# Retention chunks rotated by GpSimd during attention instead of during the retention, with the rotated keys and the queries' high and low parts passed through device memory

## The chip, the core and the metric

One core of one Trainium2 chip runs one decoder layer. The metric is the device time of one execution in microseconds (us). The kernel before was timed in three runs.

## What is computed

```python
q, k = rotary(q), rotary(k) * (RET_QK ** -0.5)         # 4 heads of 256, 1024 tokens
for chunk in 8 chunks of 128 tokens, each head:
    inner = ((qc @ kc.T) * decay_in) @ vc
    cross = (qc @ R) * xi
    R = R * gamma_c + (kc * zeta).T @ vc
    out = inner + cross
y_ret = group_norm(out) * g_ret * silu(gate_ret)
y_mla = causal_attention(q_mla, k_mla, v_mla) * silu(gate_mla)   # 8 heads, 1024 tokens
merged = sigmoid(merge_mla) * (y_mla @ w_proj_mla) + sigmoid(merge_ret) * (y_ret @ w_proj_ret)
x = rmsnorm(x + gate * (merged @ w_out))
```

## The kernel before

Every product is made of three matmuls of float32r tiles: an operand is split into a high part (ScalarE copies it with rounding) and a low part (VectorE subtracts the high part from the whole), and the low-by-low product is left out. The program is written engine by engine, with semaphores set by hand, so the order of the instructions of an engine is the order of the Python loops. The stages that matter here are these.

**Attention** (`tensor_attention`), steps g = 0 to 63, one for each head and block of 128 queries. In a step TensorE does the scores, a piece of the *fill* (the projection of the retention's values, 32 units of 24 matmuls), the transposes of the step before's probabilities, and every second step the product with the values. `FILL_STEP` says how many fill matmuls stand in each step. When a fill unit is summed, ScalarE copies it with a factor to `v_stage` (`evict_fill`, L1587), VectorE makes its low part (L1998), and GpSimd stores both, 512 KB, to `v_ret` in device memory (`store_fill`, L1286). `v_slot` chooses the place in `v_stage`: units 1 and 31 have one of their own, the others take two places in turn. `evict_fill` waits until the last store from its place has landed (`v_stored`). Besides these stores GpSimd has no work until the last two steps.

**Retention** (`tensor_retention`), steps n = 0 to 31, one for each head and chunk. SyncE loads a chunk of q and k (`qk_raw`, L969) and of the cosine and sine tables (L971), `load_qk_chunk`, four steps ahead into three places. GpSimd rotates it in `rotate_chunk`: two products of 128x512 (L1277, L1279), then a difference and a sum of 128x256 (L1281, L1282). Chunks 0 and 1 are rotated before the last attention steps, the rest during the retention, and between them GpSimd forms `token_sums` of two finished chunks' outputs (L1231 to L1238), always one rotation or more behind. ScalarE then makes the high part of the rotated q and k (`high_qk`, L1594, 128x512) and VectorE the low part (`low_qk`, L1598, 128x512). TensorE transposes the keys (`turn_keys`, L2602), forms the scores (`inner_scores`, L2615 and L2616), the outputs (`outputs`), and the state (`state`); VectorE and ScalarE normalize the output (L2137 to L2148, L1620, L1630) and TensorE transposes it (`turn_outputs`, L2660). Between these TensorE has other matmuls to do: the last fill units, then the projection of `y_mla` (`fill_set`, L2504), whose operands `y_hi`/`y_lo` and weights VectorE and ScalarE split at the same time (L2183, L616).

Of the kernel before, what the change touches and what calls it, by code (L numbers as in the profile page):

```python
# [112 lines left out]
PAIR_CHUNKS = NT // 2  # L113
GROUPS_SPLIT = ((0, 1), (2,), (3,), ())
# [34 lines left out]
class Layer:  # L149
# [3 lines left out]
    def __init__(self, nc, sem, a, t, d, out, pools):  # L153
# [72 lines left out]
        self.qk_raw = [z("qk_raw_%d" % n, kb, [P, 6, P]) for n, kb in enumerate((56, 59, 4))]  # L226
        self.qk = z("qk_chunk", 62, [P, 2, 8, P], F32R)
        self.by_sine = [z("qk_by_sine_early", 98, [P, 4, P]), z("qk_by_sine", 0, [P, 4, P])]
# [84 lines left out]
    def semaphores(self, sem):  # L313
# [14 lines left out]
        self.x_late = sem("x_t_late_ready")  # L328
# [31 lines left out]
        self.roped = sem("k_pe_roped")  # L360
# [36 lines left out]
        self.gc_loaded = [sem("gate_chunk_loaded_%d" % n) for n in range(3)]  # L397
        self.qk_step = sem("qk_rotation_step")
# [19 lines left out]
        self.t_sums_done = sem("token_sums_done")  # L418
# [20 lines left out]
        self.out_hi_ready = sem("out_w_hi_ready")  # L439
# [255 lines left out]
    def v_slot(self, unit):  # L695

        return 2 if unit in (1, FILL_UNITS - 1) else unit % 2
# [225 lines left out]
    def sync_attention(self, sp):  # L923
        d = self.d
        parts = 0
        for g in range(STEPS + 4):
# [32 lines left out]
            if g == STEPS + 2:  # L959
                self.load_qk_chunk(sp, 2)  # L960
                self.load_qk_chunk(sp, 3)
# [44 lines left out]
    def sync_retention(self, sp):  # L1006
        d = self.d
        units = 0
        for n in range(CHUNK_STEPS):
# [14 lines left out]
            if n + 4 < CHUNK_STEPS:  # L1024
                self.load_qk_chunk(sp, n + 4)
# [24 lines left out]
    def store_sums(self, sp, k):  # L1050

        h, c = k // NT, k % NT // 2
        for done, tensor, which, slot in ((2, "sums_12", self.sums_12_stored, k % 4), (4, "sums_34", self.sums_34_stored, (k - 1) % 4)):
            sp.wait_ge(self.t_sums_done, 4 * (k // 2) + done)
# [121 lines left out]
    def gpsimd(self, pool):  # L1176
# [20 lines left out]
        for r in range(R_UP, R_V):  # L1197
            kind, i = SEQ[r]
            if kind == "b":
# [4 lines left out]
                nc.gpsimd.tensor_tensor(rot[:, 3, :], rot[:, 3, :], rot[:, 1, :], ALU.add).then_inc(self.rot_added, 1)  # L1204
        units = 0
        for g in range(STEPS + 4):
            while units < self.units_filled(g - 1):
                self.store_fill(pool, units)
                units += 1
            if g == STEPS - 2:  # L1210
                for n in range(2):
                    self.rotate_chunk(pool, n)
        for n in range(2, CHUNK_STEPS):
            if n == 9:
                for unit in range(units, FILL_UNITS):
                    self.store_fill(pool, unit)
            self.rotate_chunk(pool, n)
            if n >= 4 and n % 2 == 0:
                self.token_sums(pool, n - 3)
        for k in (CHUNK_STEPS - 3, CHUNK_STEPS - 1):  # L1220
            self.token_sums(pool, k)
        self.gpsimd_output(pool)

    def token_sums(self, pool, k):

        nc = self.nc
        before = 4 * (k // 2)
# [33 lines left out]

    def rotate_chunk(self, pool, n):

        raw, late = self.qk_raw[n % 3], int(n >= 12)
        by_sine = self.by_sine[late]
        cos, sin = (raw[:, c:c + 1, :].broadcast_to([P, 4, P]) for c in (4, 5))
        pool.wait_ge(self.chunk_loaded[n % 3], 32 * (n // 3 + 1))
        if n == 0:
            pool.wait_ge(self.v_stored[2], 16)
        elif n == 12:  # L1270
            for slot in range(3):
                pool.wait_ge(self.v_stored[slot], 16 * sum(self.v_slot(unit) == slot for unit in range(FILL_UNITS)))
        if n:
            pool.wait_ge(self.qk_step, 4 * n)
        if n >= 3:
            pool.wait_ge(self.out_done, n - 2)
# [1635 lines left out]
```

## Time and profile before

| | |
|---|---|
| runs | 1587.58, 1586.52, 1585.24 us; median 1586.52 |
| profiled execution | 1586.35 us, of which the span is 1584.5 us |
| TensorE matmul busy | 1540.6 us, 97% of the span |
| VectorE, ScalarE, GpSimd busy | 994.8, 667.4, 415.9 us |
| attention | about 753 to 1075 us of the span |
| retention | about 1075 to 1340 us of the span |

A busy time is the sum of an engine's instructions; time that the sequencer spends on semaphores is not in it. Times of places are microseconds from the start of the span. The rows of the trace stand in a section of their own below.

### The profile page before, as it was taken

The numbers are of one execution on the slowest core, as the hardware profiler recorded it, in microseconds if no ns is written. First come the engines' busy times: TensorE is split into PE (matmuls) and PEld (weight loads), VectorE is DVE, ScalarE is ACT, GpSimd is POOL, SyncE is SP. The second block draws the span as 40 slices with busy tenths as digits, with TensorE's granted clock in tenths as the row PEclk, the third lists the DMA queues.
The fourth block names the chain that finished last, engine by engine and source line by source line (L and its number), as shares of the span: only waits on it lengthen the run. The fifth ranks groups of instructions, "written<-read, shape, count | busy, mean of one in ns | idle before, by whom it ended". The sixth has DMA issues, their size and how long they took to land. (4 is left out here: it accounts for less than half of the span.)

```text
span 1584.5 us, 20414 instructions
## 1 busy us (share of the span) xinstructions
PE 1540.6 (97%) x7472; PEld 1287.2 (81%) x7472; DVE 994.8 (63%) x1629; ACT 667.4 (42%) x1144; POOL 415.9 (26%) x350
## 2 busy tenths in 40 slices
PE   5999999999999999999999999999899999999998
PEld 4788888888888888788888888887677888878886
DVE  6884444444444458752666665667988877799644
ACT  7553455543333353342343343434544444445311
POOL 0032233222322200200000000017778783522000
PEclk9999999999999999999999999999999999999999
DMA  9333232333323334699365554546988787889432
GB/s 381 104 136 113 107 113 107 114 108 118 120 106 107 94 108 156 260 413 339 134 207 176 173 200 172 186 140 229 307 268 265 255 271 240 297 286 309 156 107 80
DMA packets 154499, 299.55 MB, mean 189 GB/s; under 512 B 12048, under 2 KB 93072, under 8 KB 145696
## 3 DMA queue, kind: packets, MB, share of 16 engines
q1 hardware_dynamic: 137680, 265.80, 48.5%
q10 hardware_dynamic: 12080, 15.60, 2.9%
q0 software_dynamic: 4640, 16.84, 2.7%
q8 instruction: 60, 0.98, 0.3%
q14 instruction: 39, 0.32, 0.1%
HBM read 196.23 MB, written 100.93 MB: 188 GB/s over the span
## 5 line engine op out<-in xcount | busy, mean ns | idle before, releaser
L1894 DVE TENSOR_TENSOR w_form<-w_pair,w_form 128x512 fp32r<-128x512 f32 x150 | 116.3, 776 | 124.9 <-ACT w_form L1469 123.2
L1469 ACT ACTIVATE w_form<-w_pair 128x512 fp32r<-128x512 f32 x150 | 94.7, 632 | 216.8 <-PE p_banks L2433 211.7
L1551 ACT ACTIVATE prob<-p_banks,neg_max 128x128 f32<-128x128 f32 (+3 forms) x64 | 47.4, 741 | 183.1 <-DVE neg_max L2021 183.1
L1286 POOL DMA_DIRECT2D v_ret<-v_stage x32 | 17.5, 548 | 399.8 <-DVE v_stage L1998 399.5
L2430 PE MATMUL p_banks<-h_hi,w_form 128*128 128x512 f32 x300 | 116.7, 389 | 0.0
L2432 PE MATMUL p_banks<-h_lo,w_form 128*128 128x512 f32 x300 | 116.7, 389 | 0.0
L2433 PE MATMUL p_banks<-h_hi,w_form 128*128 128x512 f32 x300 | 116.7, 389 | 0.0
L1196 POOL TENSOR_TENSOR w_pair<-w_pair 128x512 f32<-128x512 f32 x25 | 32.5, 1299 | 235.4 <-DVE w_form L1894 235.4
L2712 PE MATMUL p_banks<-t_hi,w_hi 128*128 128x512 f32 x224 | 87.5, 390 | 2.2 <-DVE t_lo L1662 2.2
L2715 PE MATMUL p_banks<-t_hi,w_lo 128*128 128x512 f32 x224 | 87.2, 389 | 0.0
L2714 PE MATMUL p_banks<-t_lo,w_hi 128*128 128x512 f32 x224 | 87.2, 389 | 0.0
L616 DVE TENSOR_TENSOR w_lo<-w_raw,w_hi 128x1024 fp32r<-128x1024 f32 (+3 forms) x63 | 66.8, 1063 | 27.7 <-ACT w_hi L595 27.0
L2472 PE MATMUL p_banks<-w_hi,h_hi 128*128 128x512 f32 x192 | 78.5, 409 | 0.6 <-DVE w_lo L616 0.6
L2430 PE MATMUL p_banks<-h_sum_hi,w_form 128*128 128x512 f32 x200 | 77.8, 389 | 0.0
L2432 PE MATMUL p_banks<-h_sum_lo,w_form 128*128 128x512 f32 x200 | 77.8, 389 | 0.0
L2433 PE MATMUL p_banks<-h_sum_hi,w_form 128*128 128x512 f32 x200 | 77.8, 389 | 0.0
L2430 PE MATMUL p_banks<-h_forms,w_form 128*128 128x512 f32 x200 | 77.8, 389 | 0.0
L2432 PE MATMUL p_banks<-h_forms,w_form 128*128 128x512 f32 x200 | 77.8, 389 | 0.0
L2433 PE MATMUL p_banks<-h_forms,w_form 128*128 128x512 f32 x200 | 77.8, 389 | 0.0
L595 ACT ACTIVATE w_hi<-w_raw 128x1024 fp32r<-128x1024 f32 (+3 forms) x63 | 53.1, 847 | 57.8 <-PE p_banks L2347 13.0
L2472 PE MATMUL p_banks<-w_lo,h_hi 128*128 128x512 f32 x192 | 76.4, 398 | 0.0
L2472 PE MATMUL p_banks<-w_hi,h_lo 128*128 128x512 f32 x192 | 76.2, 397 | 0.0
(348 smaller groups left out, 4482.7 us busy)
## 6 DMA issues: line engine op xcount, KB each, us to landing
w_pair<-in_w_pairs SPq DMA_DIRECT2D x25, 1024.0 KB, 4.8
v_ret<-v_stage POOLq DMA_DIRECT2D x32, 512.0 KB, 3.7
v_chunk<-v_ret SPq DMA_DIRECT2D x32, 512.0 KB, 3.9
w_raw<-in_w_ret SPq DMA_DIRECT2D x28, 512.0 KB, 5.5
w_raw<-in_w_dense SPq DMA_DIRECT2D x23, 512.0 KB, 5.8
act_t<-stage SPq DMA_DIRECT2D x40, 256.0 KB, 2.0
act_t<-stage_late SPq DMA_DIRECT2D x40, 256.0 KB, 2.0
ada<-in_w_ada SPq DMA_DIRECT2D x4, 2048.0 KB, 24.9
```

The costliest lines, as they stand in the source:

```text
L595: self.nc.scalar.activation(self.hi_place(r), self.split_source(r), ACT.Copy).then_inc(self.w_hi_ready, 1)
L616: self.nc.vector.tensor_tensor(self.lo_place(r), self.split_source(r), self.hi_place(r).bitcast(F32), ALU.subtract)\
L1469: self.nc.scalar.activation(self.form[f % FORM_SLOTS][:, 0, :], self.form_source(f), ACT.Copy).then_inc(self.form_hi, 1)
L1551: nc.scalar.activation(self.prob[:, g % 2, 0:width], p[:, 6:8, :].rearrange("p a n -> p (a n)")[:, 0:width], ACT.Exp, bias=self.neg_max[:, ...
L1894: nc.vector.tensor_tensor(self.form[f % FORM_SLOTS][:, 1, :], self.form_source(f), self.form[f % FORM_SLOTS][:, 0, :].bitcast(F32), ALU.su ...
L2430: self.nc.tensor.matmul(out, w_hi[:, cut], x_hi[:, q, :], start=fresh and q == 0, stop=False, skip_group_check=True)
L2432: self.nc.tensor.matmul(out, w_hi[:, cut], x_lo[:, q, :], start=False, stop=False, skip_group_check=True)
L2433: last = self.nc.tensor.matmul(out, w_lo[:, cut], x_hi[:, q, :], start=False, stop=q == KD // 2 - 1, skip_group_check=True)
L2472: ins = self.nc.tensor.matmul(self.p[:, FILL_BANKS[unit % 3], :], h[:, k, tok], w[:, cut], start=(k == 0 and kind == 0), stop=(k == KD - 1 ...
L2712: self.nc.tensor.matmul(out, self.w_hi[:, slot, cut], x_hi, start=fresh and k == 0, stop=False, skip_group_check=True)
L2714: self.nc.tensor.matmul(out, self.w_hi[:, slot, cut], x_lo, start=False, stop=False, skip_group_check=True)
L2715: done = self.nc.tensor.matmul(out, self.w_lo[:, slot, cut], x_hi, start=False, stop=k == KD - 1, skip_group_check=True)
```

## The change

All 32 rotations stand in the attention, one every second step. GpSimd loads the chunk and its tables itself (`load_rotation`, one place), rotates it, stores the rotated keys whole (`k_rot`), copies the rotated queries to their high part, stores it, subtracts, and stores the low part (`q_split`). A rotation begins when the three stores of the one before have landed (`rot_stored`), since it writes the same tiles. In the retention SyncE loads 128 KB of keys and 256 KB of query parts for a chunk, and ScalarE's and VectorE's split does the keys alone (128x256). `qk_chunk` and its key tile have three places (three in place of two, and three of a smaller size), and a chunk's load is issued three steps ahead. To make room, the fill units other than 1 and 31 share one place of `v_stage`. The reads of `qk_chunk` by TensorE take other indices and no other shapes. Two semaphores are shared in sequence with older ones.

```diff
     def v_slot(self, unit):
 
-        return 2 if unit in (1, FILL_UNITS - 1) else unit % 2
+        return 2 if unit in (1, FILL_UNITS - 1) else 0
...
     def load_qk_chunk(self, sp, n):
         if n >= 3:
+            sp.wait_ge(self.qk_lo_ready, n - 2)
             sp.wait_ge(self.k_turned, n - 2)
-            sp.wait_ge(self.qk_lo_ready, n - 2)
+            sp.wait_ge(self.out_done, n - 2)
         h, m = divmod(n, NT)
-        sp.dma_start(self.qk_raw[n % 3][:, 0:4, :].rearrange("p c n -> p (c n)"), self.d["qk"][h, m])\
-            .then_inc(self.chunk_loaded[n % 3], 16)
-        sp.dma_start(self.qk_raw[n % 3][:, 4:6, :], self.d["ret_tables"].rearrange("a p n -> p a n")[:, :, m * P:(m + 1) * P])\
-            .then_inc(self.chunk_loaded[n % 3], 16)
+        sp.wait_ge(self.rot_stored, 48 * (n + 1))
+        sp.dma_start(self.k_raw[n % 3][:, :, :], self.d["k_rot"][h, m]).then_inc(self.chunk_loaded[n % 3], 16)
+        sp.dma_start(self.qk[:, n % 3, 0:4, :].bitcast(F32).rearrange("p c n -> p (c n)"),
+                     self.d["q_split"][h, m].rearrange("p a b n -> p (a b n)")).then_inc(self.chunk_loaded[n % 3], 16)
...
         for g in range(STEPS + 4):
             while units < self.units_filled(g - 1):
                 self.store_fill(pool, units)
                 units += 1
-            if g == STEPS - 2:
-                for n in range(2):
-                    self.rotate_chunk(pool, n)
-        for n in range(2, CHUNK_STEPS):
-            if n == 9:
+            if g % 2 and g // 2 < CHUNK_STEPS:
+                self.rotate_chunk(pool, g // 2)
+        for k in range(1, CHUNK_STEPS, 2):
+            self.token_sums(pool, k)
+            if k == 3:
                 for unit in range(units, FILL_UNITS):
                     self.store_fill(pool, unit)
-            self.rotate_chunk(pool, n)
-            if n >= 4 and n % 2 == 0:
-                self.token_sums(pool, n - 3)
-        for k in (CHUNK_STEPS - 3, CHUNK_STEPS - 1):
-            self.token_sums(pool, k)
         self.gpsimd_output(pool)
...
+    def load_rotation(self, pool, n):
+        h, m = divmod(n, NT)
+        pool.dma_start(self.rot_raw[:, :, :].rearrange("p c n -> p (c n)"), self.d["qk"][h, m]).then_inc(self.rot_loaded, 16)
+        pool.dma_start(self.rot_table[:, :, :], self.d["ret_tables"].rearrange("a p n -> p a n")[:, :, m * P:(m + 1) * P])\
+            .then_inc(self.rot_loaded, 16)
+
     def rotate_chunk(self, pool, n):
...
+        pool.wait_ge(self.rot_loaded, 32 * (n + 1))
         if n == 0:
             pool.wait_ge(self.v_stored[2], 16)
...
+        else:
+            pool.wait_ge(self.rot_stored, 48 * n)
+        self.nc.gpsimd.tensor_tensor(by_sine[:, :, :], raw[:, :, :], sin, ALU.mult).then_inc(self.qk_step, 1)
+        self.nc.gpsimd.tensor_tensor(raw[:, :, :], raw[:, :, :], cos, ALU.mult).then_inc(self.qk_step, 1)
+        pool.wait_ge(self.qk_step, 6 * n + 2)
+        self.nc.gpsimd.tensor_tensor(by_sine[:, 2:4, :], raw[:, 0:2, :], by_sine[:, 2:4, :], ALU.subtract).then_inc(self.qk_step, 1)
+        self.nc.gpsimd.tensor_tensor(by_sine[:, 0:2, :], raw[:, 2:4, :], by_sine[:, 0:2, :], ALU.add).then_inc(self.qk_step, 1)
+        pool.wait_ge(self.qk_step, 6 * n + 4)
+        if n + 1 < CHUNK_STEPS:
+            self.load_rotation(pool, n + 1)
+        pool.dma_start(self.d["k_rot"][h, m], by_sine[:, 1:4:2, :]).then_inc(self.rot_stored, 16)
+        self.nc.gpsimd.tensor_copy(self.rot_q_hi[:, :, :], by_sine[:, 0:4:2, :]).then_inc(self.qk_step, 1)
+        pool.wait_ge(self.qk_step, 6 * n + 5)
+        pool.dma_start(self.d["q_split"][h, m][:, 0], self.rot_q_hi[:, :, :].bitcast(F32)).then_inc(self.rot_stored, 16)
+        self.nc.gpsimd.tensor_tensor(self.rot_q_lo[:, 0:4:2, :], by_sine[:, 0:4:2, :], self.rot_q_hi[:, :, :].bitcast(F32), ALU.subtract)\
+            .then_inc(self.qk_step, 1)
+        pool.wait_ge(self.qk_step, 6 * n + 6)
+        pool.dma_start(self.d["q_split"][h, m][:, 1], self.rot_q_lo[:, 0:4:2, :].bitcast(F32)).then_inc(self.rot_stored, 16)
...
     def high_qk(self, act, n):
-        act.wait_ge(self.qk_step, 4 * n + 4)
-        if n >= 2:
-            act.wait_ge(self.out_done, n - 1)
-        self.nc.scalar.activation(self.qk[:, n % 2, 0:4, :], self.qk_raw[n % 3][:, 0:4, :], ACT.Copy).then_inc(self.qk_hi_ready, 1)
+        act.wait_ge(self.chunk_loaded[n % 3], 32 * (n // 3 + 1))
+        if n >= 3:
+            act.wait_ge(self.out_done, n - 2)
+        self.nc.scalar.activation(self.qk[:, n % 3, 4:6, :], self.k_raw[n % 3][:, :, :], ACT.Copy).then_inc(self.qk_hi_ready, 1)
...
             if n in (2, 3):
-                dve.wait_ge(self.v_stored[1], 16 * sum(self.v_slot(unit) == 1 for unit in range(FILL_UNITS)))
+                dve.wait_ge(self.qk_step, 6 * CHUNK_STEPS)
```

GpSimd's order in the attention, before, from fill unit 2 on (`v_stage_254` and `v_stage_255` are the two places in turn):

```order
L1286 DMA v_ret<-v_stage_254 128x1024
L1286 DMA v_ret<-v_stage_255 128x1024
L1286 DMA v_ret<-v_stage_254 128x1024
L1286 DMA v_ret<-v_stage_255 128x1024
L1286 DMA v_ret<-v_stage_254 128x1024
```

The same place in the changed kernel, from the store of one fill unit to the next rotation's first instruction (`v_stage_257` is the one place; L1302 is the store of a unit, L1283 the first instruction of a rotation):

```order
L1302 DMA v_ret<-v_stage_257 128x1024 [waits v_lo_ready]
L1283 TENSOR_TENSOR qk_by_sine<-rotation_raw,rotation_table 128x512 [waits rotated_chunk_stored,rotation_chunk_loaded]
L1284 TENSOR_TENSOR rotation_raw<-rotation_raw,rotation_table 128x512
L1286 TENSOR_TENSOR qk_by_sine<-rotation_raw,qk_by_sine 128x256 [waits qk_rotation_step]
L1287 TENSOR_TENSOR qk_by_sine<-rotation_raw,qk_by_sine 128x256
L1269 DMA rotation_raw<-qk_chunks 128x512 [waits qk_rotation_step]
L1270 DMA rotation_table<-ret_tables 128x2x128
L1291 DMA k_rotated_chunks<-qk_by_sine 256x1x128
L1292 CAST rotated_q_hi<-qk_by_sine 128x256
L1294 DMA q_split_chunks<-rotated_q_hi 128x256 [waits qk_rotation_step]
L1295 TENSOR_TENSOR rotated_q_lo<-qk_by_sine,rotated_q_hi 128x2x128
L1298 DMA q_split_chunks<-rotated_q_lo 128x2x128 [waits qk_rotation_step]
```

Between two stores of fill units there now stand one or two such rotations of six operations and five DMAs. Written as S for a unit's store and R for a rotation, the changed order is SSRSRSRRSRSRRSSRRSRSRSRSRSRSRRSRSRRSSRSRSRRSRSRRSSRRSRSRSRSRSS, with 30 stores and 32 rotations; the last two stores come in the retention.

SyncE's order in the first retention steps, before and in the changed kernel (`qk_raw`/`k_raw` numbers are the three places):

```order
L986 DMA v_chunk_126<-v_ret 128x1024
L969 DMA qk_raw_121<-qk_chunks 128x512
L971 DMA qk_raw_121<-ret_tables 128x2x128
L1044 DMA y_even<-y_ret_stage_135 128x512
L994 DMA gate_chunk<-act_t 128x4x128
```

```order
L990 DMA v_chunk_129<-v_ret 128x1024
L974 DMA k_raw_120<-k_rotated_chunks 128x256
L975 DMA qk_chunk<-q_split_chunks 128x512
L1048 DMA y_even<-y_ret_stage_138 128x512
L998 DMA gate_chunk<-act_t 128x4x128
```

The two loads of a chunk keep their place in a step, and are those of the chunk three steps ahead, where they were of the one four steps ahead.

## Rows read from the trace of the kernel before

**Rows 1.** The page, busy time of the engines in the span (us, share, instructions).

```profile
PE 1540.6 (97%) x7472; PEld 1287.2 (81%) x7472; DVE 994.8 (63%) x1629; ACT 667.4 (42%) x1144; POOL 415.9 (26%) x350
```

**Rows 2.** Busy time by stretch: attention, then retention (columns in the first row).

```profile
core 0: us, PE busy (x) PEld busy (x) DVE busy (x) ACT busy (x) POOL busy (x), PEclk, DMA share, GB/s
753.00:1075.00 322.00, 321.79 (x1849) 279.43 (x1847) 205.95 (x439) 121.49 (x266) 22.99 (x35) 1.00 0.50 171
1075.00:1340.00 265.00, 252.66 (x1248) 206.08 (x1247) 215.21 (x515) 122.23 (x243) 191.59 (x187) 0.99 0.81 265
```

**Rows 3.** GpSimd in order of time: its first two stores of fill units.

```profile
759.12 1.20 POOL L1286 DMA_DIRECT2D v_ret<-v_stage  x2 [99.36 <-DVE v_stage L1998]
```

**Rows 4.** ScalarE in order of time: evictions of two close fill units, then 29.

```profile
846.21 0.68 ACT L1587 ACTIVATE v_stage<-p_banks,ret_cols 128x512 fp32r<-128x512 f32 x1
...
851.69 0.68 ACT L1587 ACTIVATE v_stage<-p_banks,ret_cols 128x512 fp32r<-128x512 f32 x1
...
1082.89 0.69 ACT L1587 ACTIVATE v_stage<-p_banks,ret_cols 128x512 fp32r<-128x512 f32 x1 [5.36 <-PE p_banks L2472]
```

**Rows 5.** Line L1286, GpSimd's stores of fill units: min/median/max ns.

```profile
L1286 POOL DMA_DIRECT2D v_ret<-v_stage x32: 531/531/883, 759.1 to 1140.9; - x32
```

**Rows 6.** DMA issues in attention, 753 to 1070: KB each, median us to landing.

```profile
v_ret<-v_stage POOLq DMA_DIRECT2D x28, 512.0 KB, 3.2
...
y_mla<-y_full SPq DMA_DIRECT2D x30, 128.0 KB, 2.7
```

**Rows 7.** Line L940, stores of y_mla: us from issue to landing, min/median/max.

```profile
DMA to landing us min/median/max: 1.7/2.7/8.3
```

**Rows 8.** GpSimd in order of time: one rotation, the next one's start.

```profile
1086.09 1.29 POOL L1277 TENSOR_TENSOR qk_by_sine_early<-qk_raw 128x512 f32<-128x512 f32 x1 [0.87 <-DMA qk_raw<-ret_tables]
1087.45 1.28 POOL L1279 TENSOR_TENSOR qk_raw<-qk_raw 128x512 f32<-128x512 f32 x1
1088.81 0.73 POOL L1281 TENSOR_TENSOR qk_raw<-qk_raw,qk_by_sine_early 128x256 f32<-128x256 f32 x1
1089.50 0.74 POOL L1282 TENSOR_TENSOR qk_raw<-qk_raw,qk_by_sine_early 128x256 f32<-128x256 f32 x1
1090.38 1.30 POOL L1277 TENSOR_TENSOR qk_by_sine_early<-qk_raw 128x512 f32<-128x512 f32 x1
```

**Rows 9.** Retention, 1090 to 1330: the rotation's second product on GpSimd (mean ns).

```profile
L1279 POOL TENSOR_TENSOR qk_raw<-qk_raw 128x512 f32<-128x512 f32 x29 | 40.3, 1390 | 2.3
```

**Rows 10.** Tile qk_raw: SyncE's issues of a chunk's two loads (ns).

```profile
L969 SPq DMA_DIRECT2D qk_raw<-qk_chunks x32: 319/320/463, 1044.2 to 1300.8; - x32
L971 SPq DMA_DIRECT2D qk_raw<-ret_tables x32: 427/435/695, 1044.6 to 1301.1; - x32
```

**Rows 11.** TensorE's wait in retention, 1075 to 1340 (us in total, times, longest).

```profile
PE p_banks L2660 <- ACT out_n L1630: 8.8, 8, 2.5
```

**Rows 12.** Busy time in two stretches of the retention.

```profile
1130.00:1140.00 10.00, 7.51 (x29) 5.73 (x29) 9.26 (x20) 5.02 (x10) 8.70 (x10) 0.83 0.64 211
...
1150.00:1160.00 10.00, 7.20 (x37) 5.57 (x38) 8.99 (x22) 4.99 (x10) 9.21 (x10) 1.00 1.00 348
```

**Rows 13.** TensorE, its longest wait there.

```profile
1132.57 0.66 PE L2660 MATMUL p_banks<-ident,out_n 128*128 128x128 f32 x4 [2.49 <-ACT out_n L1630]
```

**Rows 14.** The chain that ended last: one of its longer pieces there.

```profile
1125.17 4.47 DVE y_lo L2183 x2
```

**Rows 15.** Groups of VectorE instructions in retention, 1090 to 1330.

```profile
L1598 DVE TENSOR_TENSOR qk_chunk<-qk_raw,qk_chunk 128x512 fp32r<-128x512 f32 x30 | 28.4, 946 | 1.5 <-ACT qk_chunk L1594 1.5
...
L2118 DVE TENSOR_TENSOR k_tok<-p_banks,k_tok 128x256 fp32r<-128x256 f32 x30 | 12.5, 416 | 1.1 <-ACT k_tok L1606 1.1
```

**Rows 16.** Line L2183, VectorE: min/median/max ns.

```profile
L2183 DVE TENSOR_TENSOR y_lo<-y_raw,y_hi x8: 1214/1752/2312, 1092.1 to 1146.4; 128x1024 fp32r<-128x1024 f32 x8
```

**Rows 17.** Groups of VectorE instructions in attention, 800 to 1060.

```profile
L1998 DVE SCALAR_TENSOR_TENSOR v_stage<-p_banks,ret_cols,v_stage 128x512 fp32r<-128x512 f32 x22 | 16.4, 747 | 0.2
...
L2042 DVE TENSOR_SCALAR prob<-prob,recip 128x1024 f32<-128x1024 f32 x6 | 4.5, 754 | 0.2
```

More of the change, by code:

```diff
@@ L113 @@
 PAIR_CHUNKS = NT // 2
+SUMS_FROM, OUT_HI_FROM = 6, 11
 GROUPS_SPLIT = ((0, 1), (2,), (3,), ())
@@ L1204, in gpsimd @@
                 nc.gpsimd.tensor_tensor(rot[:, 3, :], rot[:, 3, :], rot[:, 1, :], ALU.add).then_inc(self.rot_added, 1)
+        pool.wait_ge(self.v_up_stored[2], 16 * 4)
+        pool.wait_ge(self.tables_stored, 64 + 16)
+        for slot in range(4):
+            pool.wait_ge(self.stored[slot], 16 * PAIRS)
+        pool.wait_ge(self.raw_stored, 16 * RAW)
+        self.load_rotation(pool, 0)
         units = 0
@@ L1226, in token_sums @@
         nc = self.nc
-        before = 4 * (k // 2)
+        before = SUMS_FROM + 4 * (k // 2)
         even, odd = self.y_ret[(k - 1) % 4], self.y_ret[k % 4]
@@ L1265, in rotate_chunk @@
-        by_sine = self.by_sine[late]
-        cos, sin = (raw[:, c:c + 1, :].broadcast_to([P, 4, P]) for c in (4, 5))
-        pool.wait_ge(self.chunk_loaded[n % 3], 32 * (n // 3 + 1))
+        h, m = divmod(n, NT)
+        raw, by_sine = self.rot_raw, self.by_sine
+        cos, sin = (self.rot_table[:, c:c + 1, :].broadcast_to([P, 4, P]) for c in range(2))
+        pool.wait_ge(self.rot_loaded, 32 * (n + 1))
         if n == 0:
             pool.wait_ge(self.v_stored[2], 16)
-        elif n == 12:
-            for slot in range(3):
-                pool.wait_ge(self.v_stored[slot], 16 * sum(self.v_slot(unit) == slot for unit in range(FILL_UNITS)))
@@ L1582, in evict_fill @@
                 act.wait_ge(self.split_stored[slot], self.store_count[slot])
-        elif unit == 3:
-            act.wait_ge(self.v_up_stored[2], 16 * 4)
         if self.v_stores(unit):
@@ L2601, in turn_keys @@
         for b in range(2):
-            last = self.nc.tensor.transpose(self.p[:, self.key_bank(n), b * P:(b + 1) * P], self.qk_raw[n % 3][:, 2 * b + 1, :],
+            last = self.nc.tensor.transpose(self.p[:, self.key_bank(n), b * P:(b + 1) * P], self.k_raw[n % 3][:, b, :],
                                             self.t["ident"][:, :])
@@ L2634, in outputs @@
                     pe.wait_ge(self.r_lo_ready, 2 * self.states_before(n) - 1 + b)
-                    nc.tensor.matmul(out, qk[:, 2 * b, :], self.r_hi[:, b, :], start=False, stop=False)
-                    nc.tensor.matmul(out, qk[:, 4 + 2 * b, :], self.r_hi[:, b, :], start=False, stop=False)
-                    last = nc.tensor.matmul(out, qk[:, 2 * b, :], self.r_lo[:, b, :], start=False, stop=(b == 1))
+                    nc.tensor.matmul(out, qk[:, b, :], self.r_hi[:, b, :], start=False, stop=False)
+                    nc.tensor.matmul(out, qk[:, 2 + b, :], self.r_hi[:, b, :], start=False, stop=False)
+                    last = nc.tensor.matmul(out, qk[:, b, :], self.r_lo[:, b, :], start=False, stop=(b == 1))
             last.then_inc(self.out_done, 1)
```

50 lines of the change are left out of this document (21 added, 29 removed).

## Prediction

> **What bounds the kernel now.** I read the page first: TensorE's matmuls are busy 97% of the span [rows 1], so time can only come out of what is left, or be added where TensorE is made to wait. Then busy time by stretch [rows 2]. In the attention TensorE is busy 321.8 of 322 us, GpSimd 23 of 322; in the retention TensorE is busy 252.7 of 265 us, VectorE 215 and GpSimd 192. So the attention has no idle TensorE and an idle GpSimd, and the retention has 12.3 us without a matmul. The waits [rows 11] say what most of these are: eight waits, 8.8 us, for the normalized output (L1630). Where they occur VectorE is busy 9.0 to 9.3 of 10 us [rows 12], and the chain that ended last runs through VectorE's splits of `y_mla` [rows 14]. After a wait of 2.49 us [rows 13] the granted clock of the stretch is 0.83 [rows 12]. That is the stage that the change relieves; the stage that it loads is one where nothing is left on TensorE, and all depends on whether GpSimd can do its new work in the time of the attention.
>
> The profiled execution took 1586.35 us with 1584.5 of span; the sum is made against it. The median of the runs is 0.17 us higher.
>
> **Retention: what is taken away.** VectorE's low part of a chunk takes 946 ns on the mean for 128x512 with GpSimd at work; 128x256 takes 416 in the nearest row, of another operand [rows 15]. That is 0.53 us for each of the 30 chunks there, 16 us of VectorE. GpSimd's rotations leave the stage, and with them part of what lengthens VectorE's instructions of two operands in SBUF: `y_lo` is 1214 ns at best and 1752 at the median [rows 16], 0.54 for each of 8, 4 us. ScalarE's copy halves too. The two loads keep 384 KB. All of the 12.3 us would be the upper bound, with some 3 us of low clock; nothing the lower. In ten microseconds like those of [rows 12] 1.25 chunks and one or two `y_lo` give VectorE 1.2 to 1.7 us, of 2.5 to 2.8 that TensorE misses. So I take six tenths of 12.3, 7.5 us, and 1.5 us of the clock: **9 us gained**. The loads are issued one step later; a step is 265/32 = 8.3 us, so some 12 us remain before ScalarE needs them, against landings of 3 to 4 us such as [rows 6]. I cost that, and the moved `token_sums` (less delayed than before), at nothing; without that cover ScalarE would wait in a stage where it has room.
>
> **Attention: the period of one rotation.** GpSimd's four first operations take from 1086.09 to 1090.24, 4.15 us [rows 8]; one wait between them is gone, so 4.1. A DMA issue holds GpSimd for 0.53 us [rows 5], back to back too (two in 1.20 us, [rows 3]). Three of the five move 256 pieces of 512 bytes in place of 128; on SyncE such an issue takes 427 ns against 319 [rows 10], times 1.34, so 0.71 by that ratio; bounds are 0.53 (no dearer) and 1.06 (double). The copy of 128x256 to the high part has no row on GpSimd: at most 0.73, the price of the two-operand form of that size [rows 8], at least 0.1; I take 0.42, the middle. The last subtraction is 0.73. Three waits on GpSimd's own operations cost some 0.07 each, the gap in [rows 8]. The issue of the last store then begins at 4.1 + 0.53 + 0.71 + 0.71 + 0.42 + 0.53 + 0.73 + 0.2 = 7.9 us.
>
> The next rotation waits for that store to land. The nearest row is the store of `y_mla`, also 128 KB and in this stage: 2.7 us at the median [rows 6], 1.7 at least [rows 7]. The upper bound is 3.2, of GpSimd's own stores of four times the size [rows 6]. I take 2.7: same size, same stretch. Against VectorE, the second product is 1390 ns on the mean in the retention [rows 9] and 1280 in [rows 8]; VectorE is less busy in the attention, so 0.07 for each of six operations, 0.4. Together **11.0 us a rotation**. With all lower ends it is 4.1 + 3 x 0.53 + 0.1 + 0.53 + 0.73 + 0.2 + 1.7 = 9.0, with all upper ends 8.9 + 3.2 + 0.7 = 12.8.
>
> The Trainium skill (DMA: Bandwidth & Descriptors, Anatomy of one DMA) gives a DMA of GpSimd as about 2.0 us and its bytes at 436 GB/s, 2.3 us for 128 KB. By it the period would be 10.6 and the sum below 1604.
>
> **What that does.** There are 32 rotations in about 322 us of attention, one in 10.06 us. Fill units come unevenly, two of them 5.5 us apart [rows 4]. Before, a late store harmed nobody soon; now unit n + 1 can't be evicted before unit n's store has landed, and that store stands behind one or two rotations in GpSimd's queue. Behind the waiting eviction on ScalarE stand the exponentials of the next step and the transposed probabilities, and TensorE waits for these within about 1.5 us (an estimate from [rows 2]: ScalarE and VectorE have room, TensorE has none). So GpSimd's pace becomes the pace of the stage.
>
> The first rotation waits for unit 1's store: issued by 760.3 [rows 3], landed at about 763. The last rotation has its last store issued at 763 + 32 x 11.0 - 2.0 = 1113; unit 28's store follows and lands 3.2 us later, 1116.2. Unit 29 is evicted at 1082.9 [rows 4]. Less 1.5 us, that is 31.8 us late. In three places of the order between rotations two stores stand together (RRSS): the second waits for the first to land, 3.2, and for the eviction and low part of the next unit, 0.68 [rows 4] and 0.75 [rows 17], 4.6 us, of which 2.0 pass anyway while the rotation's last store lands. That adds 3 x 2.6 = 8. **40 us lost**; in general 32 times the period less 312, which is nothing at 9.75 us. What VectorE loses to GpSimd in the attention is covered by the same wait, since TensorE is then no longer the bound; if the period is short, it costs up to 2 us.
>
> Sum: 1586.35 + 40 - 9 = **1617.4 us**.
>
> **Rivals.** (1) *GpSimd keeps pace* and the change is faster. It needs a period of 9.75 us or less: landings at 1.7 to 2 us and issues no dearer than 0.53. For it: GpSimd is idle now and the lower ends allow 9.0. Against it: every lower end but one has to hold. Then 1586.35 - 9 = 1577. Chance 0.17. The result turns from slower to faster at 9.75 + 9/32 = 10.0 us.
>
> (2) *The clock.* TensorE now waits in most rotations. In [rows 12] a wait of 2.49 us goes with 0.83 of the clock over 10 us, 1.7 us of work lost. If each rotation had this, TensorE would need 10.06 + 1.7 = 11.8 us for its share and pass GpSimd's 11.0: 25 us more at most, and with waits in three places of four 19, 1637. Chance 0.10; against it speaks that most waits would be short.
>
> (3) *Issues are held up.* The longest issue took 883 ns [rows 5]. If all five were near that, the period grows by 5 x 0.35 less what I already added, 0.54: by 1.2 us, 38 us more than my sum, 1656. The scaling of the probabilities, 754 ns for 1024 columns against 746 for 512 of a form that reads PSUM [rows 17], is the instruction that would do this. Chance 0.07, since the median equals the minimum. The Trainium skill (SBUF — State Buffer, SBUF: two separate sides) says that GpSimd can't write descriptors while VectorE runs a mode of two ports. The 883 is the only sign of it in these rows.
>
> (4) *The relief does not reach the path*: the waits for the normalized output come from the chain of small instructions, not from VectorE's load. Then the 9 us are absent, 1626. Chance 0.08.
>
> **The numbers.** My forecast, periods from 10.0 to 12.4 us with the gain, has 0.58: 1585 to 1662, its value 1617.4. The range should hold 8 in 10. Its lower end takes in rival 1, 1575; the upper end leaves out periods above about 12.2 and most of rival 3, 1655. About 0.2% of the time, 3 us, is what a measurement here can tell from no change. Faster by more is rival 1, 0.17; within it periods close to 10.0 us, 0.05; slower is the rest, 0.78.
>
> **What would show it.** In the profile after: GpSimd busy 80% or more of the attention; the time from one first product of a rotation to the next about 11 us, where under 9.8 refutes me; ScalarE's evictions (L1587) waiting for a DMA of `v_ret`; TensorE with 8 to 13% idle in the attention, which is to last about 362 us; and a retention of some 256 us with VectorE's low part near 0.42 us. An attention of 322 us would make the prediction wrong at its main step; a longer retention would make the gain wrong. If the copy or an issue of 256 pieces is far from 0.42 and 0.71, the size is off and not the mechanism.

## The result and the profile after

The changed kernel takes 1682.22 us (median of 4 runs, 1680.29 to 1685.51), the kernel before 1586.17: a ratio of 1.0607, with an interval of 1.0588 to 1.0626. It is **96 us slower**, where 31 were forecast. Busy time of TensorE in the page of the changed kernel, against [rows 1], and by stretch, against [rows 2]; the attention now ends near 1175 us:

```profile
PE 1566.7 (93%) x7472; PEld 1304.1 (78%) x7472; DVE 990.2 (59%) x1629; ACT 662.8 (39%) x1144; POOL 545.9 (32%) x574
```

```profile
753.00:1175.00 422.00, 350.40 (x1878) 299.51 (x1877) 224.03 (x439) 122.21 (x265) 289.74 (x373) 0.91 0.57 191
1175.00:1440.00 265.00, 254.95 (x1254) 207.86 (x1253) 200.26 (x518) 120.15 (x247) 57.72 (x75) 0.99 0.81 273
```

The attention takes 422 us in place of 322, with a granted clock of 0.91, and TensorE is idle for 72 of them. The matmuls of the stage are the same ones but for some 30 at the border; its busy time of 350 us in place of 322 goes with the lower clock. The second row is as wide as that of [rows 2] and so says nothing of how long the retention is; it is read below. GpSimd in the attention, by line (L1283 to L1287 are the rotation, L1292 and L1295 the query parts, the DMA lines the five issues and L1302 the stores of the fill units):

```profile
L1284 POOL TENSOR_TENSOR rotation_raw<-rotation_raw,rotation_table 128x512 f32<-128x512 f32 x32 | 43.5, 1360 | 0.0
L1283 POOL TENSOR_TENSOR qk_by_sine<-rotation_raw,rotation_table 128x512 f32<-128x512 f32 x32 | 41.2, 1289 | 79.5 <-DMA q_split_chunks<-rotated_q_lo 72.1 <-DMA v_ret<-v_stage 7.4
L1286 POOL TENSOR_TENSOR qk_by_sine<-rotation_raw,qk_by_sine 128x256 f32<-128x256 f32 x32 | 26.5, 829 | 2.5
L1287 POOL TENSOR_TENSOR qk_by_sine<-rotation_raw,qk_by_sine 128x256 f32<-128x256 f32 x32 | 24.9, 779 | 0.0
L1295 POOL TENSOR_TENSOR rotated_q_lo<-qk_by_sine,rotated_q_hi 128x256 fp32r<-128x256 f32 x31 | 24.1, 777 | 0.3
L1298 POOL DMA_DIRECT2D q_split_chunks<-rotated_q_lo x31 | 22.9, 739 | 9.5 <-POOL rotated_q_lo L1295 9.5
L1291 POOL DMA_DIRECT2D k_rotated_chunks<-qk_by_sine x31 | 22.7, 731 | 1.4 <-issue 1.4
...
L1292 POOL CAST rotated_q_hi<-qk_by_sine 128x256 fp32r<-128x256 f32 x31 | 16.7, 537 | 0.0
L1302 POOL DMA_DIRECT2D v_ret<-v_stage x28 | 15.6, 557 | 23.9 <-DVE v_stage L2012 23.7
```

Here 32 first products had 79.5 us of idle time before them, nearly all for the landing of the rotation's last store. One rotation in order of time, to the next one's first product:

```profile
905.73 1.28 POOL L1283 TENSOR_TENSOR qk_by_sine<-rotation_raw,rotation_table 128x512 f32<-128x512 f32 x1 [1.10 <-DMA q_split_chunks<-rotated_q_lo]
906.98 1.29 POOL L1284 TENSOR_TENSOR rotation_raw<-rotation_raw,rotation_table 128x512 f32<-128x512 f32 x1
908.34 0.74 POOL L1286 TENSOR_TENSOR qk_by_sine<-rotation_raw,qk_by_sine 128x256 f32<-128x256 f32 x1
909.04 0.73 POOL L1287 TENSOR_TENSOR qk_by_sine<-rotation_raw,qk_by_sine 128x256 f32<-128x256 f32 x1
910.07 0.61 POOL L1269 DMA_DIRECT2D rotation_raw<-qk_chunks  x1 [0.30 <-POOL qk_by_sine L1287]
910.66 0.72 POOL L1270 DMA_DIRECT2D rotation_table<-ret_tables  x1
911.38 0.73 POOL L1291 DMA_DIRECT2D k_rotated_chunks<-qk_by_sine  x1
911.99 0.54 POOL L1292 CAST rotated_q_hi<-qk_by_sine 128x256 fp32r<-128x256 f32 x1
912.82 0.56 POOL L1294 DMA_DIRECT2D q_split_chunks<-rotated_q_hi  x1 [0.30 <-POOL rotated_q_hi L1292]
913.40 0.76 POOL L1295 TENSOR_TENSOR rotated_q_lo<-qk_by_sine,rotated_q_hi 128x256 fp32r<-128x256 f32 x1
914.46 0.74 POOL L1298 DMA_DIRECT2D q_split_chunks<-rotated_q_lo  x1 [0.30 <-POOL rotated_q_lo L1295]
915.19 0.56 POOL L1302 DMA_DIRECT2D v_ret<-v_stage  x1
919.81 1.28 POOL L1283 TENSOR_TENSOR qk_by_sine<-rotation_raw,rotation_table 128x512 f32<-128x512 f32 x1 [4.06 <-DMA q_split_chunks<-rotated_q_lo]
```

The last store is issued 8.73 us after the first product, and the next rotation starts 5.35 us after that. The first products begin at 767.5 and end at 1171.3 (31 periods, the line L1283), so a period is 13.0 us on the mean. The landing of that last store over the whole run, from the start of its issue:

```profile
DMA to landing us min/median/max: 2.2/2.4/8.1
```

And who waited in the attention (us in total, times, longest):

```profile
ACT v_stage L1601 <- DMA v_ret<-v_stage: 87.7, 15, 12.0
DVE v_stage L2012 <- ACT v_stage L1601: 82.2, 13, 11.7
POOL qk_by_sine L1283 <- DMA q_split_chunks<-rotated_q_lo: 72.1, 28, 7.5
...
PE p_banks L2594 <- DVE pt_lo L2066: 33.7, 5, 11.1
```

ScalarE's evictions of fill units waited 15 times for a unit's store, 87.7 us, VectorE's low part waited behind them, and TensorE waited five times, 33.7 us, for the low part of the probabilities, which VectorE makes behind that. That is the chain that the prediction named.

### The profile page after: what moved, and what is told of

The parts are those of the page before. It is cut to its first block, busy times and chain, and to the rows that moved or that the text cites. A ratio compares the mean times of both kernels' runs of the same rounds, so it can differ in the third digit from the quotient of the medians.

```text
span 1680.2 us, 20667 instructions
## 1 busy us (share of the span) xinstructions
PE 1566.7 (93%) x7472; PEld 1304.1 (78%) x7472; DVE 990.2 (59%) x1629; ACT 662.8 (39%) x1144; POOL 545.9 (32%) x574
## 4 chain that ended last, share of the span: by engine, by line
PE 58%; POOL 17%; DMA 11%; DVE 6%; issue 5%; ACT 2%; SPq 0%; ACTq 0%; POOLq 0%; DVEq 0%
PE p_banks L2446 9%; PE p_banks L2447 9%; PE p_banks L2444 9%; DMA q_split_chunks<-rotated_q_lo 6%; PE p_banks L2518 4%; POOL rotation_raw L1284 3%; PE p_banks L2359 2%; PE p_banks L2361 2%; PE p_banks L2360 2%; POOL qk_by_sine L1283 2%; PE p_banks L2757 2%; PE p_banks L2756 2%; PE p_banks L2755 2%; POOL qk_by_sine L1286 2%; POOL rotated_q_lo L1295 1%
## 5 line engine op out<-in xcount | busy, mean ns | idle before, releaser
L2728 PE MATMUL p_banks<-t_lo,w_hi 128*128 128x512 f32 x224 | 87.7, 392 | 0.0
L2729 PE MATMUL p_banks<-t_hi,w_lo 128*128 128x512 f32 x224 | 87.7, 392 | 0.0
L2486 PE MATMUL p_banks<-w_hi,h_hi 128*128 128x512 f32 x192 | 82.0, 427 | 0.6 <-DVE w_lo L620 0.6
L2486 PE MATMUL p_banks<-w_hi,h_lo 128*128 128x512 f32 x192 | 79.9, 416 | 0.0
L2594 PE MATMUL p_banks<-ident,prob 128*128 128x128 f32 x288 | 46.8, 294 | 33.7 <-DVE pt_lo L2066 33.7
L2572 PE MATMUL p_banks<-pt_hi,v_head 128*128 128x256 f32 (+1 forms) x160 | 46.4, 290 | 33.8 <-issue 17.7
```

The lines of the kernel that those rows point to most:

```text
L2486: ins = self.nc.tensor.matmul(self.p[:, FILL_BANKS[unit % 3], :], h[:, k, tok], w[:, cut], start=(k == 0 and kind == 0), stop=(k == KD - 1 ...
L2728: self.nc.tensor.matmul(out, self.w_hi[:, slot, cut], x_lo, start=False, stop=False, skip_group_check=True)
L2729: done = self.nc.tensor.matmul(out, self.w_lo[:, slot, cut], x_hi, start=False, stop=k == KD - 1, skip_group_check=True)
```

## The experiments

The delay is read at one place in every kernel: the start of the first output matmul of the retention (L2629 before, L2643 after). The retention is read from there to the last transposes of an output (L2660 before). Each reading is from one profiled execution. The runs of one kernel lie up to some 12 us apart (no_stores, 1602.88 to 1614.56), so a difference of a few us between two kernels in this table is only a sign. For the kernel before, then the changed one:

```profile
L2629 PE MATMUL p_banks<-v_chunk,inner_hi x32: 389/395/721, 1082.7 to 1328.0; 128*128 128x512 f32 x32
```

```profile
L2660 PE MATMUL p_banks<-ident,out_n x128: 270/272/330, 1088.2 to 1335.4; 128*128 128x128 f32 x128
```

```profile
L2643 PE MATMUL p_banks<-v_chunk,inner_hi x32: 389/395/501, 1178.5 to 1419.9; 128*128 128x512 f32 x32
```

```profile
L2674 PE MATMUL p_banks<-ident,out_n x128: 270/272/328, 1189.3 to 1427.3; 128*128 128x128 f32 x128
```

So the attention ends 95.8 us later, the retention takes 248.8 us in place of 252.7, 3.9 less, and the stages behind it 252.9 in place of 249.1, 3.8 more. The same three readings for every kernel:

| kernel | time, us | first output, us | against before | first output to last transposes |
|---|---|---|---|---|
| before | 1586 | 1082.7 | | 252.7 |
| one_place | 1593.07 | 1089.5 | +6.8 | 252.9 |
| one_place_sync | 1588.78 | 1082.7 | 0.0 | 255.7 |
| no_stores | 1610.82 | 1116.2 | +33.5 | 243.7 |
| constant_source | 1634.10 | 1137.9 | +55.2 | 245.3 |
| changed kernel | 1682.22 | 1178.5 | +95.8 | 248.8 |
| sync_stores | 1663.76 | 1094.6 | +11.9 | 318.3 |
| half_early | 1592.47 | 1094.4 | +11.7 | 244.9 |
| half_early_sync | 1580.71 | 1083.9 | +1.2 | 244.7 |
| ten_early_sync | 1580.99 | 1084.9 | +2.2 | 244.8 |

For twentyone_early_sync (1580.22) and half_early_sync_again (1579.81), below, the times are given alone; the profiled execution of the first, 1584.58 us, was the slowest of its ten.

**Theory A** is that of the prediction: one place of `v_stage`, whose stores stand behind rotations in GpSimd's queue, makes GpSimd's lateness that of ScalarE and TensorE. **The rivals** are that the one place does it alone (B), that the added traffic and the port which GpSimd shares with VectorE do it (C), and that other waits do (D).

### one_place: the single place alone

```diff
-        return 2 if unit in (1, FILL_UNITS - 1) else unit % 2
+        return 2 if unit in (1, FILL_UNITS - 1) else 0
```

VectorE's third and fourth output of the retention, which waited for the stores from the place that is gone, wait for that of unit 1.

> The kernel before with one edit: the fill units other than 1 and 31 share one place of v_stage. Theory A (the loss is the product of two things, one place and a slow queue in front of its stores): alone the single place costs almost nothing, since a store lands 3.2 us after its issue and the closest units are 5.5 us apart; 1586 to 1588 us. Rival B (the single place is enough by itself to hold up ScalarE): several of the 28 evictions wait 1 to 3 us, 1600 to 1640 us.

Ratio 1.0038 (1.0026 to 1.005): 6 us, more than A said and less than B. The waits from 753 to 1095:

```profile
ACT v_stage L1587 <- DMA v_ret<-v_stage: 14.3, 3, 7.9
...
PEld p_banks L2539 <- ACT prob L1551: 4.8, 9, 2.3
```

Three evictions waited. Two of them, 6.4 us together and 4.1 at most, come before the first output at 1089.5, and so belong to its delay; the one of 7.9 us is over at 1092.2, behind it. The store for which the eviction at 855.4 waited took 6.1 us to land, among a head's loads of 7.7 and 4.3 us. My 3.2 us for a landing was a median, and it is the long ones that count.

### constant_source: no wait for the landing

```diff
-            pool.wait_ge(self.rot_stored, 48 * n)
+            pool.wait_ge(self.qk_step, 6 * n)
...
-        pool.dma_start(self.d["k_rot"][h, m], by_sine[:, 1:4:2, :]).then_inc(self.rot_stored, 16)
+        same = self.t["ident"][:, :].rearrange("p (a n) -> p a n", a=1).broadcast_to([P, 2, P])
+        pool.dma_start(self.d["k_rot"][h, m], same).then_inc(self.rot_stored, 16)
```

The other two stores read the same constant, so the device memory holds no rotated chunks, and the issue of the query's high part has 256 pieces too.

> The changed kernel, but the three stores of a rotation read a constant tile in place of the rotated ones, so that the next rotation need not wait for their landing (the stored values are not the rotated ones; every instruction and DMA is still issued, with 256 pieces for all three stores). Theory A: the period falls from 13.0 us by the 4.1 us between the issue of the last store and the next rotation, to 8.9 + 0.7 for the issue and 0.6 for a unit's store, 10.2; the attention then loses 32 x 10.2 - 312 = 14 us by the sum of the prediction, in all 1590 to 1605 us. Rival C (the traffic or the port shared with VectorE slows the stage, not the wait): the stores and the operations are all there, so it stays above 1650 us.

1634.1 us in its one run, 48 us below the changed kernel, and its first output 40.6 us earlier: the wait for the landing is the largest part of the loss, and C, which wanted more than 1650, falls as the main cause. But 55 us of delay remain where A's sum had 14. Many periods are the 10.2 us that A expected (L1283), but their mean is 11.5: rotations waited 15.1 us for their own loads, and GpSimd 18 us for fill units that were not ready.

### no_stores: the rotations' operations and loads, without their stores

```diff
-            pool.wait_ge(self.rot_stored, 48 * n)
+            pool.wait_ge(self.qk_step, 6 * n)
...
-        pool.dma_start(self.d["k_rot"][h, m], by_sine[:, 1:4:2, :]).then_inc(self.rot_stored, 16)
...
-        sp.dma_start(self.k_raw[n % 3][:, :, :], self.d["k_rot"][h, m]).then_inc(self.chunk_loaded[n % 3], 16)
+        sp.dma_start(self.k_raw[n % 3][:, :, :].rearrange("p c n -> p (c n)"), self.d["qk"][h, m][:, 0:2 * P]).then_inc(self.chunk_loaded[n % 3], 16)
```

The load of the query parts likewise reads the unrotated chunk.

> The changed kernel without the three stores of a rotation; the retention loads the same number of bytes from the unrotated chunks (so the result is computed from other values). Theory A: a rotation takes about 7 us of GpSimd and never holds up the stage; the attention is back at 322 us and the whole retention relief shows: 1577 us if my 9 us were right, 1582 if it is the 4 us that the retention of the changed kernel was shorter by. Rival C: rotations still stand against VectorE in the attention, so 1586 or more.

Ratio 1.0133 (1.0095 to 1.0172), 1610.8 us: neither figure of A, and what C said, 1586 or more. Its retention takes 243.7 us, 9.0 less than before: the relief that I had summed. The attention, though, is 33.5 us longer with rotations that take GpSimd some 7 us of every 11. Its waits, from 753 to 1075:

```profile
POOL v_ret L1299 <- DVE v_stage L2009: 68.1, 14, 11.1
...
POOL qk_by_sine L1283 <- DMA rotation_table<-ret_tables: 29.6, 13, 6.3
...
ACT v_stage L1598 <- DMA v_ret<-v_stage: 26.6, 7, 4.9
...
PEld p_banks L2550 <- ACT prob L1564: 10.8, 12, 3.7
```

GpSimd waits for work 14 times, 68 us in all (11 of them before the first rotation), so it is not the bound on the mean. And still ScalarE waits for a unit's store seven times here, and eight up to the first output: a unit that becomes ready while a rotation (or two) stands before its store is stored that much later. It could be this, or C; the next run tells.

### sync_stores: the unit's stores out of the rotations' queue

```diff
+            while units < self.units_filled(g - 1):
+                self.store_fill(sp, units)
+                units += 1
```

These lines move from GpSimd's loop to the head of a step of SyncE's, and the last two stores with them. VectorE's third output waits for the last rotation's stores to land, where it waited for its last operation.

> The changed kernel, with the stores of the fill units issued by SyncE instead of GpSimd, so that the one place no longer depends on the rotations; the stores of the rotated chunks and their wait remain, and VectorE's third output still waits for the last rotation. Theory A: the attention is back at about 322 us, rotations go on into the retention until 763 + 32 x 12.4 = 1160 us, and the retention stands still at its third chunk, due at about 1100, until then: 1586 + 60 - 4, 1635 to 1650 us, with the idle time of TensorE in one piece. Rival D (rotations and the stage slow each other through TensorE's waits for other things): the attention stays well above 350 us.

1663.8 us in one run. The first output:

```profile
L2643 PE MATMUL p_banks<-v_chunk,inner_hi x32: 389/395/500, 1094.6 to 1405.6; 128*128 128x512 f32 x32
```

It is 11.9 us late in place of 95.8, although 24 of the 32 rotations have begun by then, 13.3 us apart as in the changed kernel (13.0), with their stores and loads. **This settles it for A**: taking the stores out of the queue removes 84 of the 96 us, and C and D have the 12 that are left. ScalarE no longer waits for a store in the attention. Of the 12 us, 5.5 are waits of TensorE that the kernel before has not, for a load of values under the added traffic:

```profile
PE p_banks L2572 <- DMA v_head<-v_hl: 5.5, 3, 4.6
```

C is bounded from another side too. Up to the first output VectorE is busy 209.4 us in the kernel before, 220.1 here and 226.3 in the changed kernel, so what GpSimd's operations add to VectorE's is 17 us there and 11 here. The rest of the time is the stop that was foretold, where VectorE's third output waits for the last rotation, whose tiles lie in the same place:

```profile
1110.00:1180.00 70.00, 10.96 (x55) 8.85 (x53) 4.74 (x14) 4.06 (x8) 49.42 (x65) 0.59 0.34 112
1180.00:1420.00 240.00, 220.40 (x1082) 179.13 (x1083) 175.76 (x461) 101.36 (x213) 55.03 (x72) 0.96 0.79 261
```

TensorE is busy 11 of 70 us, and the granted clock of that stretch is 0.59, between its two levels of 1.2 and 2.4 GHz. The total is 14 us over the top of what I expected, since the last rotation began at 1182.5 and not at some 1150. The first one began at 768.8, 1.3 us later than in the changed kernel and 6 later than I had put it; the rest, some 29 us, is the period, 13.3 us where I expected 12.4. The landings of the last store summed to 112.8 us of GpSimd's idle time, 31 times, against 72 in the changed kernel, where a unit's store often filled part of that wait:

```profile
L1283 POOL TENSOR_TENSOR qk_by_sine<-rotation_raw,rotation_table x32: 1252/1281/1838, 768.8 to 1182.5; 128x512 f32<-128x512 f32 x32
...
  DMA q_split_chunks<-rotated_q_lo: 112.8, 31
  DMA v_ret<-v_stage: 18.5, 1
```

### Fewer rotations, written back whole

`one_place_sync` is `one_place` with SyncE's stores. `half_early` rotates chunks 0 to 15 in the attention, one in four steps, and writes each back with one DMA; the retention loads it and splits 128x512 as before:

```diff
+            if g % EVERY == 1 and g // EVERY < EARLY:
+                self.rotate_chunk(pool, g // EVERY)
+            if g % EVERY == EVERY - 1 and g // EVERY + 1 < EARLY:
+                self.load_rotation(pool, g // EVERY + 1)
...
+        if n < EARLY:
+            h, m = divmod(n, NT)
+            pool.wait_ge(self.qk_step, 4 * n + 4)
+            pool.dma_start(self.d["qk"][h, m], raw[:, 0:4, :].rearrange("p c n -> p (c n)")).then_inc(self.rot_stored, 16)
```

`half_early_sync` adds SyncE's stores of the fill units to that; `ten_early_sync` does 10 chunks, one in six steps; `twentyone_early_sync` 21, one in three.

> The kernel before with the one place of v_stage, and the stores of the fill units issued by SyncE in place of GpSimd, no other edit. In one_place two evictions waited, 4 us at most, and the time rose by 6 us. If it is the landing of a store amid other loads that costs this, whoever issues it, 1590 to 1594 us; if SyncE issues it ahead of the head's loads (its order puts the unit's store first in a step) the wait goes, 1586 to 1589 us.

Ratio 1.0014 (1.0003 to 1.0025), at the edge of no change, and its first output at 1082.7, as before: no eviction waits for a store any more. Its retention is 3.0 us longer, 255.7; why was not tried. In the attention the landing of a unit's store from there is 2.7 us at the median, where GpSimd's was 3.1 in one_place.

> The kernel before, but chunks 0 to 15 are rotated in the attention, one in four steps (20 us), and written back whole with one store; the retention loads them rotated and splits queries and keys as before; chunks 16 to 31 are rotated in the retention. One place of v_stage, stores by GpSimd. Theory A (a unit's store standing behind a rotation): a rotation without the query split takes about 6 us of GpSimd and its landing is waited for by nobody soon, so only the stores that fall behind one are late; attention plus 6 (one place) plus 5 to 10, retention minus 5 to 7 since the first half has no rotations: 1588 to 1600 us. If the average rate alone counted, as in the sum of the prediction, the attention would lose only the 6 us: 1585 to 1588.

Ratio 1.004 (1.0027 to 1.0052), 1592.5 us. The attention loses 11.7 us, 4.9 more than with the place alone, although a rotation starts only every fourth step, some 20 us apart, and takes GpSimd some 6 (its four operations and three issues). The average rate is not what counts; four evictions wait for a store, where one_place has two up to its first output:

```profile
POOL v_ret L1311 <- DVE v_stage L2023: 177.5, 27, 11.1
...
ACT v_stage L1612 <- DMA v_ret<-v_stage: 11.8, 4, 5.3
...
PE p_banks L2583 <- DVE pt_lo L2077: 4.4, 1, 4.4
```

> half_early with the stores of the fill units issued by SyncE. Theory A: the rotations no longer stand in front of the stores; attention plus 1 to 4 us, retention minus 5 to 7: 1580 to 1586 us, faster than the kernel before or equal to it. Rival C (traffic and the shared port slow the attention by themselves): no better than half_early.

Ratio 0.996 (0.9945 to 0.9975), 1580.71 us: **faster than both kernels**, by 0.4% against the one before. The rows of its two stages, with the border moved to 1085:

```profile
753.00:1085.00 332.00, 331.41 (x1902) 287.27 (x1902) 213.93 (x449) 123.65 (x271) 95.62 (x110) 1.00 0.59 203
1085.00:1340.00 255.00, 247.44 (x1225) 201.70 (x1224) 207.06 (x509) 123.82 (x242) 125.09 (x129) 1.00 0.82 277
```

TensorE is idle for 0.6 us of the attention, and GpSimd does 96 us of work there in place of 23, with the first output 1.2 us later. From its first output to its last transposes the retention takes 8.0 us less, though all of it still splits 128x512: nearly all of the 9.0 us of no_stores can be had without the halved split, by taking the rotations out of the first half alone. The halved split by itself was not run.

> half_early_sync with chunks 0 to 9 rotated in the attention, one in six steps, and 10 to 31 in the retention. Nearly all of TensorE's waits of the retention stand in its first nine chunks, so most of the relief should stay: 1580 to 1586 us, within 2 us of half_early_sync. If the relief needs GpSimd idle throughout, it is 3 us or more above it.

Ratio 0.9962 (0.9947 to 0.9977), 0.3 us from half_early_sync: ten chunks are enough. Fewer were not tried.

> half_early_sync with chunks 0 to 20 rotated in the attention, one in three steps (15 us), where half_early_sync has 16 and one in four. With SyncE's stores the rotations stand in front of nothing, and a rotation with its landing and the next load takes some 12 us, so it still fits; TensorE has little left to wait for in the second half of the retention: 1579 to 1583 us, the same within 2 us. If the added traffic and VectorE's longer instructions begin to count in the attention, 1584 or more.

Ratio 0.9962 (0.9951 to 0.9973), 1580.22 us; the same again.

> half_early_sync once more with more rounds, to place it against the kernel before: ratio 0.996 again, 1580 to 1582 us. If the first measurement was luck, within 0.2% of the kernel before.

Ratio 0.9957 (0.9941 to 0.9973), 1579.81 us. The gain of 6 us stands.

## Why the prediction was wrong

**Right:** the direction, the mechanism and its chain. GpSimd can't do a rotation in two steps of attention, and the one place passes its lateness to ScalarE and TensorE. sync_stores shows this by taking the chain apart.

**Wrong: the period of one rotation**, 11.0 us in the sum and 13.0 measured. Its terms, the means taken over the 31 periods:

| term | in the sum | measured |
|---|---|---|
| first product to the issue of the last store | 7.9, with VectorE's share 8.3 | 8.7 in a quiet period, 9.1 on the mean |
| of it: copy to the high part | 0.42 | 0.54 |
| of it: issue of 256 pieces; of 128 | 0.71; 0.53 | 0.72 to 0.74; 0.56 to 0.60 |
| of it: wait for GpSimd's own last operation before a DMA | 0.07 | 0.30, three times |
| issue of the last store to the next rotation | 2.7 | 2.6 at the median, 3.9 on the mean |
| the same in the three places where two stores stand together | 2.7 + 2.6 | 6.1 each |
| the same in the other 28 | 2.7 | 3.7 on the mean |

The issues were sized well by SyncE's ratio, and an undisturbed period is near the sum: the rotations that begin at 767.46 and 894.21 are followed by the next after 11.1 and 11.5 us. Two terms failed. The larger is the step "2.7 us at the median [rows 6]", short by 1.0 us a rotation: the median of the last store's landing is even lower, 2.4 us, but the longest is 8.1, and a chain in which each rotation waits for each landing adds up means, not medians. I had the 8.3 us of [rows 7] before me and used that line for its minimum only. The smaller is GpSimd's own work, short by 0.8 us a rotation, of which 0.7 are the three waits before a DMA, put at 0.07 and measured at 0.30. 32 times these 1.8 us are 58 us of delay, and the measured delay is 56 over the sum's 40. The 8 us for two stores together were sized well: GpSimd waited three times for a unit between rotations, 4.2 us each.

With 13.0 us in place of 11.0 the formula of the prediction gives 32 x 13.0 - 312 = 104 us of delay. But its 312 holds the 8 us for two stores together, which the measured mean has in it already; without them it gives 96, against 95.8 measured. That it comes so near is partly chance, since the first rotation began 4.5 us later than the formula has it. For no_stores, where GpSimd waits for work, the sum of the prediction gives nothing at all with the 7 us that a rotation takes, and the run has 33.5 us. **The second step that failed is "so GpSimd's pace becomes the pace of the stage", taken as the only cost:** a store behind a rotation delays its unit even when the queue has time to spare. The increments of the first output, in the order one_place, no_stores, constant_source, changed kernel, are 6.8 us for the one place, 26.7 for the rotations and their loads before the stores, 21.7 for issuing their own stores with the traffic of these, and 40.6 for the wait for landings. The middle two are not parted further by any run, and each is worth what it is only in this order.

**The 9 us of gain in the retention** were right in size: no_stores has 9.0, half_early_sync 8.0. In the changed kernel 3.9 are left. An eviction at its start still waited for a store, and TensorE behind VectorE's low part of that unit, 3.6 us of the 5.1 that are missing:

```profile
1184.32 0.69 ACT L1601 ACTIVATE v_stage<-p_banks,ret_cols 128x512 fp32r<-128x512 f32 x1 [6.01 <-DMA v_ret<-v_stage]
...
1185.93 0.55 PE L2629 MATMUL p_banks<-qk_chunk 128*128 128x256 f32 x1 [3.63 <-DVE v_stage L2012]
```

Another 3.8 us went behind the retention, where TensorE waits 3.7 us for `t_lo`, in place of 1.5, and the granted clock from 1492 to 1542 is 0.97. Why these come there I did not try.

**The rivals.** Rival 1 (GpSimd keeps pace) fell with the rotation at 8.7 us before any landing, and the shortest landing at 2.2. Rival 2 (the clock) is half true: the clock is 0.91 in the attention and costs 28 us of TensorE's busy time, but in a stage in which it is waiting anyway; no run separates what of it reached the end. Rival 3 (issues held up) is refuted by L1298, 739 to 748 ns in 32 issues; the longest of all five kinds is 835. Rival 4 (no relief) is refuted by the 9.0 us of no_stores. Of the signs that I named, ScalarE's waits were there, and VectorE's low part near 0.42 us (0.44); the idle TensorE was too, with 17% in place of 8 to 13, and the retention was shorter, by 3.9 us in place of 9. GpSimd's 80% was not there: it was busy 290 of 422 us, 69%, since landings are idle time for it.

Two small slips of the working: with the period of 10.6 its sum is 1604.6, not below 1604; and the chance of 0.05 is said to lie within the 0.17 of rival 1, but the 0.78 for slower counts it beside.

**VectorE's instructions** did get longer in the attention, with GpSimd at work. Its low part of a weight before, and in the changed kernel the scaling of probabilities at 1024 columns, 754 ns before [rows 17], and that low part:

```profile
L616 DVE TENSOR_TENSOR w_lo<-v_weight_raw_odd,w_hi 128x1024 fp32r<-128x1024 f32 x6 | 7.3, 1224 | 0.6 <-ACT w_hi L595 0.3
```

```profile
L2056 DVE TENSOR_SCALAR prob<-prob,recip 128x1024 f32<-128x1024 f32 x5 | 5.1, 1021 | 0.2
```

```profile
L620 DVE TENSOR_TENSOR w_lo<-v_weight_raw_odd,w_hi 128x1024 fp32r<-128x1024 f32 x6 | 12.7, 2110 | 0.4
```

The Trainium skill (SBUF — State Buffer, Who interferes with whom) says that an instruction of VectorE in a mode of two ports, and one with two inputs in SBUF if GpSimd's reads SBUF, block or are blocked by GpSimd's for the whole instruction. The longer low part and scaling agree; three low parts of another tile (`w_lo_aside`), 1222 ns before and 1223 after, show no blocking. It is a large effect on single instructions and a small one on the time: 17 us of VectorE's busy time in all, in a stage in which it has room, and sync_stores has 11 of these and a delay of 11.9 us.

## What to carry to other kernels

Before giving an idle engine more work, look at what already stands in its queue: a 0.5 us DMA issue that frees a buffer did no harm here on an empty queue with two places, and becomes the pace of the kernel behind 9 us of work, more so if the buffer is made single to find room. Move the releasing DMA to another queue first (here worth 84 us of delay at the first output, of which the whole kernel kept 18, as the retention then waited for the last rotation), then ask for the mean landing of a store that the next round waits for, not its median. And take only the part of the work that is worth moving: ten of the 32 chunks gave as much, 6 us, as 16 or 21.

## What the runs showed that I had not expected

- A DMA of GpSimd that waits for GpSimd's own last operation starts 0.30 us after it; one that follows without a wait starts at once, and an operation after an operation with a wait starts 0.07 us after it [rows 8].
- In the attention of the changed kernel the landing of a 128 KB store is 2.2 to 8.1 us with a median of 2.4. Long ones stand in the stretches of a head's loads, which come back every 45 to 65 us there.
- GpSimd's issue of 256 pieces takes 0.72 to 0.74 us on the mean against 0.56 to 0.60 for 128, a ratio near SyncE's [rows 10].
- Moving the unit's stores from GpSimd to SyncE made them land sooner (2.7 us against 3.1 at the median, in the attention) and removed the 6.8 us that the single place had cost at the first output; of its 6 us of the whole time 2 are left.
